# Adding up the squares of each RMS norm on GpSimd, with one ones-matmul for a norm

## The reference

```python
def rmsnorm(x, g):
    xf = x.astype(F32)
    y = xf * lax.rsqrt(jnp.mean(xf * xf, axis=-1, keepdims=True) + EPS)
    return (y * g.astype(F32)).astype(x.dtype)
...
h = h + rms_norm(mix @ w_out[l], ln_attn_post[l])
hn = rms_norm(h, ln_ffn_pre[l])
```

## Time and profile before

| what | value |
|---|---|
| three runs, device time | 2542.32, 2543.93, 2549.96 us; median 2543.93 |
| the profiled execution | span 2542.3 us; the page gives no other time for it |
| TensorE busy | 2328.3 us, 92% of the span, mean granted clock 0.919 |
| VectorE, ScalarE, GpSimd busy | 975.5, 749.4, 150.4 us |
| DMA | 155.70 MB, 61 GB/s over the span |
| ones-matmuls (L1615) | 154 records, two to a matmul; 3.1% of the chain |
| flip matmuls of even (L1815) | in the chain from 144.1 us |

### The profile page before, as it was taken

The page is one execution under the profiler, slowest core; times in us unless marked ns, Lnnn a source line. Parts: engine busy times, 40 slices in busy tenths (PEclk is TensorE's granted clock), DMA queues, the critical chain, the costliest instruction groups (busy, mean ns, idle before and its releaser), DMA issues.

```text
span 2542.3 us, 26867 instructions
## 1 busy us (share of the span) xinstructions
PE 2328.3 (92%) x10863; PEld 1848.5 (73%) x10863; DVE 975.5 (38%) x1341; ACT 749.4 (29%) x1106; POOL 150.4 (6%) x127
## 2 busy tenths in 40 slices
PE   7999999999997899899999898957889978999997
PEld 4865768887865777688878587836777855888785
DVE  4322432222334664322233434464222145555434
ACT  3134322222233544322222324242111123333321
POOL 2000000000001110100000110002211201000000
PEclk9989599999998999999999998978767789999998
DMA  5300023222221110222322130200000011233220
GB/s 158 100 17 1 1 66 100 90 91 99 93 67 39 36 51 28 72 90 91 99 89 94 51 109 1 89 27 1 1 1 1 1 47 46 90 99 99 83 99 33
DMA packets 120385, 155.70 MB, mean 61 GB/s; under 512 B 3176, under 2 KB 108656, under 8 KB 120176
## 3 DMA queue, kind: packets, MB, share of 16 engines
q1 hardware_dynamic: 119008, 152.51, 18.6%
q0 software_dynamic: 1296, 2.05, 0.3%
HBM read 152.44 MB, written 2.11 MB: 61 GB/s over the span
## 4 chain that ended last, share of the span: by engine, by line
PE 86%; DVE 9%; ACT 3%; issue 1%; DMA 1%; POOL 1%; SPq 0%; POOLq 0%; ACTq 0%; DVEq 0%
PE bank L1844 28%; PE bank L1625 15%; PE bank L1862 14%; PE bank L1615 3%; PE bank L1685 3%; PE bank L1713 3%; PE bank L1634 3%; PE bank L2032 2%; PE bank L2040 2%; PE bank L1701 2%; PE bank L1750 2%; PE bank L2045 1%; DVE arena L1098 1%; PE bank L1738 1%; PE bank L2071 1%
## 5 line engine op out<-in xcount | busy, mean ns | idle before, releaser
L1844 PE MATMUL bank<-XH,w_hi 128*128 128x512 f32 x1056 | 420.2, 398 | 19.2 <-POOL XL L679 18.6
L1844 PE MATMUL bank<-XH,w_lo 128*128 128x512 f32 x1056 | 414.1, 392 | 0.0
L1844 PE MATMUL bank<-XL,w_hi 128*128 128x512 f32 x1056 | 413.8, 392 | 0.0
L1625 PE MATMUL bank<-XH,w_hi 128*128 128x512 f32 x584 | 240.3, 411 | 43.0 <-POOL XL L679 18.2
L1844 PEld LDWEIGHTS bank<-XH,w_hi 128*128 128x128 f32 x1056 | 199.6, 189 | 68.3 <-issue 16.7
L1625 PE MATMUL bank<-XH,w_lo 128*128 128x512 f32 x584 | 233.8, 400 | 0.0
L1625 PE MATMUL bank<-XL,w_hi 128*128 128x512 f32 x584 | 233.5, 400 | 0.0
L1844 PEld LDWEIGHTS bank<-XH,w_lo 128*128 128x128 f32 x1056 | 199.2, 189 | 42.3
L1844 PEld LDWEIGHTS bank<-XL,w_hi 128*128 128x128 f32 x1056 | 199.8, 189 | 40.0
L1862 PE MATMUL bank<-XH,w_hi 128*128 128x512 f32 x528 | 207.7, 393 | 9.9 <-DVE XL L1268 9.9
L1862 PE MATMUL bank<-XL,w_hi 128*128 128x512 f32 x528 | 207.2, 392 | 0.0
(11 more groups left out here) (272 smaller groups left out, 3370.5 us busy)
## 6 DMA issues: line engine op xcount, KB each, us to landing
w_raw<-in_ffn_w_gate SPq DMA_DIRECT2D x22, 1024.0 KB, 5.3
w_raw<-in_ffn_w_up SPq DMA_DIRECT2D x22, 1024.0 KB, 5.4
w_raw<-in_ffn_w_down SPq DMA_DIRECT2D x22, 1024.0 KB, 5.0
w_raw<-in_w_up SPq DMA_DIRECT2D x22, 1024.0 KB, 5.0
w_raw<-in_w_in SPq DMA_DIRECT2D x13, 1024.0 KB, 5.3
w_raw<-in_w_down SPq DMA_DIRECT2D x11, 1024.0 KB, 4.9
w_raw<-in_even_w_in SPq DMA_DIRECT2D x9, 1024.0 KB, 5.3
w_raw<-in_even_w_out SPq DMA_DIRECT2D x4, 1024.0 KB, 5.2
```

The costliest lines, as they stand in the source:

```text
L1625: m = pe.matmul(bank[L % 4][0:M, :], cols(w, k), x[:, x0 + k, :], start=(first_k and k == 0 and j == 0), stop=(last_k and k == kt - 1 and ...
L1844: m = pe.matmul(bank[b][:, :], w[:, k, P * c:P * (c + 1)], x[:, k, :], start=(k == 0 and j == 0), stop=(k == KT - 1 and j == 2))
```

## The change

The squares are no longer summed by TensorE alone. GpSimd gets `square_sum`: it copies square 0 to `NTMP[:, 0, :]` and adds the others to it, one by one, each add waiting for the one before; `sq_used` is now raised by GpSimd. TensorE waits for the last of them and multiplies that one tile by ones; a new semaphore `ss_ready` tells ScalarE. `norm_split` calls `square_sum` first, and `fnorm`, `post` and `fpost`, which have no split, call it by itself. In even the norm's GpSimd work moves ahead of the store of the bias row.

```diff
             def norm_split(name):
                 use, t0, tiles, src, col, gain, done = norm_plan(name)
+                square_sum(name)
                 for k in range(0, tiles, 2):
...
+            def square_sum(name):
+                use, t0, tiles, src, col, gain, done = norm_plan(name)
+                for k in range(tiles):
+                    pool.wait_ge(sq_ready, t0 + k + 1)
+                    if k == 0:
+                        pool.tensor_copy(NTMP[:, 0, :], NS[:, 0, :]).then_inc(sq_used, 1)
+                    else:
+                        pool.wait_ge(sq_used, t0 + k)
+                        pool.tensor_tensor(NTMP[:, 0, :], NTMP[:, 0, :], NS[:, k % 2, :], ALU.add).then_inc(sq_used, 1)
...
                 pool.dma_start(tabx[0:32, :], d["rel_bias_table"]).then_inc(side_loaded, 16)
+                norm_split("even")
                 pool.wait_ge(bias_row_ready, 1)
                 pool.dma_start(scratch, brow[0:8, 0:384]).then_inc(bias_out, 16)
-                norm_split("even")
                 pool.wait_ge(bias_out, 16)
...
+                if s == "fnorm":
+                    square_sum("fnorm")
...
+                    square_sum("post")
+            square_sum("fpost")
...
-                act.wait_ge(sq_used, t0 + tiles)
+                act.wait_ge(ss_ready, use + 1)
                 link(act.activation(rstd, bank[7][:, :], ACT.Ln, bias=epsb[:, 0:1]))
...
-                for k in range(tiles):
-                    pe.wait_ge(sq_ready, t0 + k + 1)
-                    pe.matmul(bank[7][:, :], C("ones"), NS[:, k % 2, :], start=(k == 0), stop=(k == tiles - 1))\
-                      .then_inc(sq_used, 1)
+                pe.wait_ge(sq_used, t0 + tiles)
+                pe.matmul(bank[7][:, :], C("ones"), NTMP[:, 0, :], start=True, stop=True).then_inc(ss_ready, 1)
```

More of the change, by code:

```diff
@@ L259, in build @@
         sq_used = sem("sq_used")
+        ss_ready = sem("ss_ready")
         rstd_ready = sem("rstd_ready")
```

## The result

The changed kernel takes 2555.31 us (median of 4 runs, 2553.95 to 2560.02), the kernel before, timed beside it, 2543.12 (4 runs, 2542.25 to 2549.96). The ratio is 1.0051, 95% interval 1.0035 to 1.0066: slower, by more than the 0.3% that this measurement can tell. The forecast was 2558.0, range 2546 to 2572. The profiled execution spans 2553.6 us against 2542.3, that is +11.3 where the sum said +14.1.

What follows compares the result with a forecast made beforehand. The prediction took TensorE, 86% of the chain, to bound the kernel. Shifts of Ln, norm by norm, summed to +14.1 us: 2542.3 + 14.1 = 2556.4, or 2558.0 against the median of 2543.93; range 2546 to 2572.

Steps and rivals of the forecast that it cites:

- even: Norm even: copy held by VectorE's weight split until 21.52, Ln at 33.8 in place of 28.94, +4.9 us.
- The add, 1.35: Each GpSimd add of a square: 1.35 us per step, waiting for the add before; low end 1.26, high end 1.55.
- dearer step of 1.55: Rival: the 59 adds standing in the open take 1.55 us each, 12 us more, 2570 us; chance 0.15.
- pre: Norm pre: five adds taking turns with VectorE at 1.75 us each, then two at 1.35; Ln +5.3 us.
- The copy, 0.7: GpSimd's copy of the first square in each norm: 0.7 us, the middle between 0.1 and 1.27.
- The last matmul at low clock, 2.15: After TensorE's pause: from last add to Ln 1.22 + 0.93 = 2.15 us; 1.22 if the clock hasn't fallen.
- Blocking: GpSimd adds and VectorE instructions with two SBUF inputs take turns, 7.05 us in fpre; rival without it 2543.8 us, chance 0.12.
- fpre: Norm fpre, the dearest: GpSimd's steps stop VectorE while it produces X's tiles; Ln +9.9 us.
- Code load in the open: Rival: up to 9.0 us of preparation for GpSimd's first tensor_tensor exposed in even; 2562.5 with half, 2567 with all; chance 0.18.
- Moved steps at nothing: In even, bias store and eight reloads go behind the norm's split: costed at nothing, about 5 us without cover.
- linear-fed norms: ffn0, ffn1 and post: squares ready early, under the last linear unit; Ln -1.9 us each, -5.8 for three.
- down-fed: mla, fnorm and fpost: VectorE feeds the tiles late, reading PSUM without being blocked; Ln +0.5 us each, +1.4 together.

Runs made afterwards that it cites:

- e4_warm: Changed kernel plus 4 to 17 overwritten ones-matmuls of constants by norm, ahead of TensorE's wait for the sum: 2549.22 us, ratio 1.0030.
- e5_late: Changed kernel, but in pre and fpre GpSimd starts only when VectorE has made all eight tiles: 2560.91 us (one run).
- e3_quarter: Changed kernel with adds covering 128 of 512 columns, so part of the sum is left out: 2510.98 us (one run).
- e6_order: Changed kernel with the bias store back ahead of even's norm on GpSimd's queue: 2556.81 us (one run).
- b_again: The unchanged kernel before, traced a second time on another chip: 2540.19 us (one run).
- e1_four: Changed kernel with GpSimd summing only in ffn0, q, ffn1 and post; other norms and bias store as before the change: 2532.72 us, ratio 0.9965.
- e7_split: e1_four, plus GpSimd summing squares 0 to 3 in mla, fnorm and fpost, TensorE taking that sum and squares 4 to 7: 2527.82 us, ratio 0.9941.
- a_again: The changed kernel, unaltered, traced a second time on another chip: 2553.19 us, ratio 1.0050.

## Why the prediction was right, and where its terms were off

Timeline of norm even in the changed kernel, which answers to the earlier trace rows:

```profile
20.17 1.13 ACT L784 ACTIVATE arena<-X 128x512 f32<-128x512 f32 x2
...
20.46 2.29 DVE L1101 TENSOR_TENSOR w_lo<-w_raw,w_hi 128x2048 fp32r<-128x2048 f32 x1
...
20.85 2.38 POOL L681 COPY arena<-arena 128x512 f32<-128x512 f32 x1 [18.37 <-ACT arena L784]
...
23.38 9.69 POOL L684 TENSOR_TENSOR arena<-arena 128x512 f32<-128x512 f32 x7 [0.16 <-POOL arena L681]
...
33.13 2.07 PE L1630 MATMUL bank<-arena,con 128*128 128x512 f32 x2 [11.75 <-POOL arena L684]
35.24 0.69 ACT L787 ACTIVATE arena<-bank,small 128x512 f32<-128x512 f32 x1 [4.25 <-PE bank L1630]
```

- **The add, 1.35.** Measured 1.40 to 1.45 from start to start where nothing holds it. Seven take 9.69 to 9.83 us instead of 9.45, and 0.15 more pass between the copy and the first. This makes mla, fnorm and fpost +0.95 instead of +0.5, and ffn0 and ffn1 -1.6 instead of -1.9. The dearer step of 1.55 is excluded where VectorE rests; in pre, where the engines take turns, a step was 1.67, not the 1.75 of the forecast, which is most of pre's +4.8 for +5.3.
- **The copy, 0.7.** 0.61 alone. That the middle between two far bounds lay so near was luck. Behind a weight split it ends 0.5 us after the split, where 0.7 was reckoned. The estimate from the Trainium skill's one-input rate (GPSIMD Engine Reference, Engine selection), 0.43 us plus start-up, would leave 0.18 us for the start-up, which no run here shows by itself.
- **The last matmul at low clock, 2.15.** Right in nine norms, Ln 2.2 us after the last add. The others are q, where TensorE comes later than the sum, and post, where the matmul took 1.10 us and the price is -2.53 instead of -1.9; it makes up for ffn0 and ffn1, so that the three together came out as forecast. e4_warm gave the microsecond back by keeping TensorE busy.
- **Blocking.** Shown by e5_late (9.77 us back to 5.39) and e3_quarter (1.75 down to 0.94). The form was right, the size too high: fpre's X7 came 5.6 us later, not 7.05. A held instruction loses 1.0 to 1.07 us, not a whole add of 1.27, since part of it passes beside GpSimd's work, and the copy costs 0.35, not 0.7. Five times 1.04 and 0.35 make 5.55. This is the mis-sized term of fpre, +8.45 for +9.9.
- **Code load in the open.** Fell. The configuration stands at 23.2 us, and the first add starts 0.16 us after the copy, the same in e6_order. The nine microseconds of the earlier trace rows were no preparation. The Trainium skill's 6 us for the first call of a freshly loaded kernel (GPSIMD Engine Reference, Instruction dispatch) appear in neither trace at this place.
- **Moved steps at nothing.** Right. The store is issued at 48.15 us, the last reload ends at 54.4, and the first reader comes near 150. e6_order shows that the new order gains 1.3 us, which even's +4.9 contains without naming it: that norm was reckoned with the copy free to start at the end of the split.
- **The sum.** +14.1 measured for +14.1, but by terms that cancel: linear-fed norms -5.7 (-5.8), down-fed +2.85 (+1.4), q and kv -1.5 (-1.6), even +5.15 (+4.9), pre +4.8 (+5.3), fpre +8.45 (+9.9). The total is better than its parts were, and that it fits to a tenth is luck; the mechanisms are what held. The span's remaining -2.7 us are within what happens without any change: b_again's span is 3.9 us shorter than the first trace's.
- **The range.** The forecast's own 2551 to 2565 doesn't follow from the bounds named for it: nine last matmuls at full clock alone would be 8 us less, 2550. The measured 2555.31 lies well inside either.

**Even's price is the least certain.** Its eight matmuls run at whatever clock is granted so early. First square to Ln with TensorE summing took 9.92 us in the kernel before (granted clock 0.83), 10.50 in b_again, 11.69 in e1_four and 8.40 in e7_split. The windows over that norm in e1_four:

```profile
20.20:31.90 11.70, 11.59 (x18) 3.81 (x18) 2.75 (x2) 4.94 (x9) 0.52 (x1) 0.71 0.29 92
```

and in e7_split:

```profile
18.90:27.20 8.30, 8.13 (x18) 2.46 (x16) 2.75 (x2) 4.86 (x9) 0.52 (x1) 1.00 0.45 139
```

So even costs 3.4 to 6.7 us by the base one picks; 5.15 is the first pair of traces, and a_again against b_again gives 4.48.

## What to carry to other kernels

Moving a reduction from a bottleneck engine to an idle one pays only where the idle engine works in the bottleneck's shadow: here where TensorE still had matmuls of the stage before to finish. Where the tiles arrive last, compare step against step (1.41 us for a GpSimd add, 0.96 for the ones-matmul), and look at what the other engine does to the producer of the tiles: beside a VectorE operation with two SBUF inputs each GpSimd add of 512 columns costs VectorE about a microsecond (0.26 us with 128 columns), and nothing was lost where VectorE read PSUM. Decide it place by place: kept to four of eleven places the change makes the kernel 0.35% faster; with a divided sum in three more it measured 0.6%, but the norms' own prices give the divided sum only 2.6 us, 0.1%.

## What was not expected of the hardware

TensorE's clock after a pause is not the same from place to place and from one execution to the next. Windows over the last matmul of ffn0 and of post in the changed kernel:

```profile
373.90:376.00 2.10, 2.04 (x2) 0.50 (x2) 0.00 (x0) 0.00 (x0) 0.00 (x0) 0.50 0.00 0
2119.50:2120.65 1.15, 1.10 (x2) 0.29 (x2) 0.00 (x0) 0.00 (x0) 0.00 (x0) 0.99 0.00 0
```

Before the first TensorE was idle for 3.90 us, before the second for 3.92, and both follow the last linear unit; one ran at 1.2 GHz and the other at 2.4. In e1_four ffn0's ran at the high level after 3.92 us. In e7_split mla's fell to the low one after 0.82, fpost's stayed at the high one after 0.81. What decides it stays open. Stretches that the change doesn't touch differ by up to 6 us, nearly half of what the change costs, and in the one looked at above the granted clock differs with them (0.828 and 0.847), so the price of an edit of this size is better read norm by norm than from two spans.
